# Expert places of 64 and 32 rows taken in two chunks of 1792 columns, and the places paired in another order

## The reference

```python
logits = xt @ w_router + b_router
top_v, top_i = lax.top_k(logits, 2)
gates = softmax(top_v)
combine = einsum('tk,tke->te', gates, one_hot(top_i, 8))
for e in range(8):
    out = out + combine[:, e:e+1] * ((silu(xt @ w_gate[e]) * (xt @ w_up[e])) @ w_down[e])
```

## Time and profile before

| | us |
|---|---|
| median of 3 runs (1421.67 to 1425.79) | 1423.94 |
| the profiled execution's own time | 1424.28 |
| its span | 1422.3 |
| TensorE busy | 1331.0 (94%) |
| VectorE busy | 466.4 (33%) |
| ScalarE busy | 279.3 (20%) |
| moved by DMA | 423.50 MB, mean 298 GB/s |

### The profile page before, as it was taken

The page is one execution under the profiler, slowest core; times in us unless marked ns, Lnnn a source line. Parts: engine busy times, 40 slices in busy tenths (PEclk is TensorE's granted clock), DMA queues, the critical chain, the costliest instruction groups (busy, mean ns, idle before and its releaser), DMA issues.

```text
span 1422.3 us, 18648 instructions
## 1 busy us (share of the span) xinstructions
PE 1331.0 (94%) x7762; PEld 753.4 (53%) x7762; DVE 466.4 (33%) x1035; ACT 279.3 (20%) x519; POOL 98.4 (7%) x115
## 2 busy tenths in 40 slices
PE   6989999999899979999999999999999999987775
PEld 5846599999684655454554444453433344332322
DVE  7998865554678541130101010110110100100002
ACT  3542444342263100000011010110110101000001
POOL 4530000000451000000000000000000000000000
PEclk9999999999899989999999999999999999999999
DMA  9433344438032288899999868989999999999994
GB/s 308 141 119 118 119 178 178 178 128 315 2 98 79 78 327 309 321 414 411 412 414 410 358 261 360 391 339 411 410 415 411 410 416 411 411 415 412 411 415 197
DMA packets 126734, 423.50 MB, mean 298 GB/s; under 512 B 21632, under 2 KB 23864, under 8 KB 118456
## 3 DMA queue, kind: packets, MB, share of 16 engines
q1 hardware_dynamic: 121464, 421.75, 75.7%
q10 hardware_dynamic: 5184, 0.52, 0.4%
HBM read 421.20 MB, written 1.05 MB: 297 GB/s over the span
## 4 chain that ended last, share of the span: by engine, by line
PE 74%; DMA 14%; DVE 8%; issue 1%; SPq 1%; ACT 1%; POOL 0%; DVEq 0%; ACTq 0%
PE psall L2349 14%; DMA m_ring<-in_moe_w_down_dram 12%; PE psall L2443 11%; PE psall L2364 8%; PE psall L2381 6%; PE psall L2054 4%; PE psall L2454 3%; PE psall L2269 3%; PE psall L2152 3%; PE psall L2271 3%; PE psall L2270 3%; PE psall L2218 2%; PE psall L2320 2%; PE psall L2481 2%; PE psall L2416 2%; PE psall L2251 1%
## 5 line engine op out<-in xcount | busy, mean ns | idle before, releaser
L2364 PE MATMUL psall<-m_ring,xeT 128*64 128x448 f32 x1024 | 202.5, 543 | 22.7 <-DMA m_ring<-in_moe_w_up_dram 21.6
L2443 PE MATMUL psall<-m_ring,hidT 128*64 128x512 f32 (+1 forms) x672 | 201.0, 597 | 17.1 <-DMA m_ring<-in_moe_w_down_dram 16.2
L2349 PE MATMUL psall<-m_ring,xeT 128*128 128x448 f32 x512 | 194.4, 540 | 0.0
L2364 PEld LDWEIGHTS psall<-m_ring,xeT 128*64 128x64 f32 x1024 | 73.5, 137 | 140.0 <-issue 139.0
L2349 PEld LDWEIGHTS psall<-m_ring,xeT 128*128 128x128 f32 x512 | 96.6, 190 | 92.4 <-issue 92.2
L2443 PEld LDWEIGHTS psall<-m_ring,hidT 128*64 128x64 f32 (+1 forms) x672 | 72.6, 154 | 136.2 <-issue 120.1
L1938 DVE TENSOR_TENSOR hid<-e_silu,psall 64x448 f32<-64x448 f32 x32 | 19.9, 623 | 354.6 <-ACT e_silu L1271 352.5
L1619 DVE TENSOR_TENSOR w_lo<-ring,w_hi 128x1024 fp32r<-128x1024 f32 x66 | 80.4, 1224 | 67.8 <-ACT w_hi L1215 67.8
L2381 PE MATMUL psall<-m_ring,xeT 128*32 128x448 f32 x1024 | 102.0, 542 | 0.0
L2269 PE MATMUL psall<-hnT_hi,w_hi 128*128 128x256 f32 x352 | 99.7, 283 | 0.7 <-DVE hnT_lo L1757 0.7
L2271 PE MATMUL psall<-hnT_hi,w_lo 128*128 128x256 f32 x352 | 99.5, 283 | 0.0
(11 more groups left out here) (327 smaller groups left out, 1454.7 us busy)
## 6 DMA issues: line engine op xcount, KB each, us to landing
m_ring<-in_moe_w_gate_dram SPq DMA_DIRECT2D x128, 896.0 KB, 20.1
m_ring<-in_moe_w_up_dram SPq DMA_DIRECT2D x128, 896.0 KB, 17.1
m_ring<-in_moe_w_down_dram SPq DMA_DIRECT2D x64, 1792.0 KB, 19.2
ring<-in_w_in_dram SPq DMA_DIRECT2D x10, 2048.0 KB, 12.8
ring<-in_ffn_w_gate_dram SPq DMA_DIRECT2D x5, 2048.0 KB, 10.4
ring<-in_ffn_w_up_dram SPq DMA_DIRECT2D x5, 2048.0 KB, 7.6
ring<-in_ffn_w_down_dram SPq DMA_DIRECT2D x5, 2048.0 KB, 7.8
ring<-in_w_out_dram SPq DMA_DIRECT2D x4, 2048.0 KB, 8.0
```

Of the source, the lines that this page charges most:

```text
L2349: ins = M(m_bank(key)[:, 0:MH], x[:, i, 0:P], weights(kind, i, s), start=(i == 0), stop=(i == KT - 1))
L2364: ins = M(m_bank(key)[64 * n:64 * n + 64, 0:MH], x[:, i, 0:64], weights(kind, i, s), start=(i == 0), stop=(i == KT - 1))
L2443: ins = M(y, hidT[:, r, 0:shape[0]], rows(r, 512 * n, 512), **ends)
```

## The change

Places of 64 and 32 rows (D and E) are now **narrow**: they have 2 chunks of 1792 columns instead of 4 of 896. A gate or up load of theirs is one row tile of 128 rows by 1792 columns, still one slot, so its rows are 7 KB instead of 3.5 KB; a turn of theirs has 16 slots of gate and up and 8 of down. The down loads keep their 14 KB rows, and A, B and C keep theirs of all kinds. The products are the same in number and size, but the side-by-side halves are now the two 896-column halves m of the chunk, and gate and up lie in banks of their own (`halves`, `halves_down`). So the hidden values of a D turn are 128 rows, of an E turn 64, and one set of 7 transposes serves a chunk of double width. The pairs are now (A,E), (D,D), (B,E), (C,D): "AEDDBECD". Turns: a pair whose first place is wide (A, B or C) goes 0,0,1,0,0,1, the pair (D,D) goes 0,1,0,1, 22 turns in all. The release of narrow units is one row tile of gate and up at a time. The path for further rows of an overfull expert (`NI`, not taken with this input) follows suit and is left out below.

```diff
-ITEMS = "AEBECDDD"
+ITEMS = "AEDDBECD"
...
+NARROW = 2
+MN = NARROW * MW
+TURNS = [(0, 1) * NARROW if CAPS[i] <= 64 else (0, 0, 1) * NARROW for i in range(0, NI, 2)]
+PICKS_AT = [1 if len(a) == 2 * NARROW else 2 for a in TURNS]
...
-        if pos == 2:
-            then = [("pt", p)]
-        if pos == 6 and 2 * p + 2 < NI:
-            first, then = [("xg", 2 * p + 2, 0)], [("xg", 2 * p + 2, 1)]
+        if pos == PICKS_AT[p]:
+            then = then + [("pt", p)]
+        if pos == FIRST_DONE[p] - 1 and 2 * p + 2 < NI:
+            first, then = first + [("xg", 2 * p + 2, 0)], then + [("xg", 2 * p + 2, 1)]
...
+    def narrow(self, it):
+        return self.shape(it) in ((64,), (32,))
+
+    def chunks(self, it):
+        return MC // NARROW if self.narrow(it) else MC
...
-        for base, rows in self.row_tiles(it):
+        for base, rows in [(0, NARROW * self.tokens(it))] if self.narrow(it) else self.row_tiles(it):
...
+        if self.narrow(it):
+            for i in range(KT - 1):
+                self.event(("kh", it, c, i))
+            if shape[0] == 64:
+                for kind, s, who, bank in (("g", 0, "A", 0), ("g", 1, "A", 1), ("u", 0, "V", 2),
+                                           ("u", 1, "V", self.misc())):
+                    self.add((kind, it, c, s), who, bank)
+            else:
+                for kind, who in (("g", "A"), ("u", "V")):
+                    self.add((kind, it, c, 0), who, self.rolling())
+            last = ("u", it, c, 1 if shape[0] == 64 else 0)
+            for i in range(KT):
+                for kind in "gu":
+                    self.load(it, c, kind, i, last if i == KT - 1 else ("kh", it, c, i))
+            return
...
+        if self.narrow(it):
+            for m in range(NARROW):
+                ends = keys and m == NARROW - 1
+                self.load(it, c, "d", 2 * m, ("dh", it, c, m))
+                self.load(it, c, "d", 2 * m + 1, keys[0] if ends else ("dn", it, c, m))
+                self.event(("dh", it, c, m))
+                if ends:
+                    self.add(keys[0], "A", keys[0][2])
+                else:
+                    self.event(("dn", it, c, m))
+            return
...
-                a = c * MW
+                narrow = experts.narrow(it)
+                a = c * (MN if narrow else MW)
                 if kind == "d":
+                    a, half = a + h // 2 * MW, h % 2
                     src = moe_w_down[0, e, a:a + MW, :].rearrange("e (p r) n -> p (e r n)", r=MB)
-                    sp.dma_start(unit(it, c, kind, h), src[:, h * DOWN * UNIT:(h + 1) * DOWN * UNIT]).then_inc(full, 16)
+                    sp.dma_start(unit(it, c, kind, h),
+                                 src[:, half * DOWN * UNIT:(half + 1) * DOWN * UNIT]).then_inc(full, 16)
+                elif narrow:
+                    src = (moe_w_gate if kind == "g" else moe_w_up)[0, e, h * P:(h + 1) * P, a:a + MN]
+                    sp.dma_start(unit(it, c, kind, h), src.rearrange("e p n -> p (e n)")).then_inc(full, 16)
...
+                if shape == (32,):
+                    m_arrived(act, ("g", it, c, 0), k)
+                    nc.scalar.activation(e_silu[:, 2, :], m_bank(("g", it, c, 0))[:, 0:MH],
+                                         ACT.Silu).then_inc(m_drained["A"], 1)
+                    return
...
+                    b = m_bank(("u", it, c, 0))
+                    for m in range(NARROW):
+                        for s in range(2):
+                            q = slice(64 * m + 32 * s, 64 * m + 32 * s + 32)
+                            ins = V.tensor_tensor(hid[32 * m:32 * m + 32, s * MH:(s + 1) * MH], e_silu[q, 2, :],
+                                                  b[q, 0:MH], ALU.mult)
+                    ins.then_inc(m_drained["V"], 1)
+                    return
...
+                def halves():
+                    one = 1 if shape[0] == 64 else 0
+                    for i in range(KT):
+                        tokens_in(i)
+                        for kind in "gu":
+                            unit_wait(pe, it, c, kind, i, k)
+                            w = unit(it, c, kind, i)
+                            for s in range(2):
+                                key = (kind, it, c, s * one)
+                                if i == 0 and (one or not s):
+                                    m_open(pe, key, k)
+                                for m in range(NARROW):
+                                    q = 64 * m if one else 64 * m + 32 * s
+                                    ins = M(m_bank(key)[q:q + shape[0], 0:MH], x[:, i, 0:shape[0]],
+                                            w[:, m * MW + s * MH:m * MW + (s + 1) * MH], start=(i == 0),
+                                            stop=(i == KT - 1))
+                                if i == KT - 1 and (one or s):
+                                    event(ins)
+                        if i < KT - 1:
+                            event(ins)
...
+                        if i < KT - 1:
+                            event(ins)
...
+            def halves_down(it, c, k):
+
+                n = experts.tokens(it)
+                lane = experts.lane(it)
+                last = c == experts.chunks(it) - 1
+                opens = c == 0 and not (n == 32 and lane and experts.shares(it))
+                wide = 512 if n == 64 else 256
+                for m in range(NARROW):
+                    for r in range(MB):
+                        if r in (0, 3):
+                            unit_wait(pe, it, c, "d", 2 * m + r // 3, k)
+                        ends = dict(start=(opens and m == 0 and r == 0), stop=(last and m == NARROW - 1 and r == MB - 1))
+                        for q in range(DM // wide):
+                            a = r * DM + q * wide
+                            big = DOWN * UNIT
+                            w = unit(it, c, "d", 2 * m + a // big)[:, a % big:a % big + wide]
+                            y = ps[5 + lane][64 * q:64 * q + 64, :] if n == 64 else \
+                                ps[7][32 * q:32 * q + 32, 256 * lane:256 * lane + 256]
+                            ins = M(y, hidT[:, r, n * m:n * m + n], w, **ends)
+                        if r in (3, MB - 1):
+                            event(ins)
```

More of the change, by code:

```diff
@@ L117, in __init__ @@
         self.add(("pt", NI // 2), "A", self.misc())
-        for c in range(MC):
+        for c in range(self.chunks(NI)):
             self.gate_up(NI, c)
@@ L122, in __init__ @@
             self.turned(NI, c)
-        self.down(NI, MC - 1)
+        self.down(NI, self.chunks(NI) - 1)
         self.scatter(NI // 2, range(4))
@@ L1262, in silus @@
                 shape = experts.shape(it)
+                if shape == (32,):
[3 more added lines that the diff above has]
+                    return
                 if shape[0] > 32:
                     for s in range(2):
-                        if shape[0] == P:
+                        if shape[0] == P or experts.narrow(it):
                             m_arrived(act, ("g", it, c, s), k)
@@ L1331, in _ @@
                     picks_out(NI // 2, k)
-                    for c in range(MC):
+                    for c in range(experts.chunks(NI)):
                         silus(NI, c, k)
@@ L1928, in hidden @@
                 shape = experts.shape(it)
+                if shape == (32,):
+                    m_wait_drained(dve, ("g", it, c, 0), k)
+                    m_arrived(dve, ("u", it, c, 0), k)
+                    b = m_bank(("u", it, c, 0))
[6 more added lines that the diff above has]
+                    return
                 for s in range(2):
                     cols = slice(s * MH, (s + 1) * MH)
-                    if shape[0] == P:
+                    if shape[0] == P or experts.narrow(it):
                         m_wait_drained(dve, ("g", it, c, s), k)
@@ L1972, in _ @@
                         choose(nxt, slice(nxt, nxt + 1))
[L1973 removed]
+                if pos == FIRST_DONE[p] - 1 and p + 1 < NI // 2:
                     take_tokens(2 * p + 2)
@@ L2385, in quad @@
                     return ins
-                if shape[0] == P:
+                if experts.narrow(it):
+                    halves()
+                elif shape[0] == P:
                     for kind in "gu":
@@ L2406, in hidden @@
                 shape = experts.shape(it)
-                last = ("w", it, c) if 32 in shape else ("u" if shape[0] == P else "gu", it, c, 1)
+                last = ("u", it, c, 0 if shape == (32,) else 1) if shape[0] == P or experts.narrow(it) else ("w", it, c)
+                if len(shape) > 1:
+                    last = ("w", it, c)
                 m_wait_drained(pe, last, k)
@@ L2424, in down @@
                 m_wait_drained(pe, ("tr", it, c, len(experts.r_pieces(it)) - 1), k)
-                last = c == MC - 1
+                last = c == experts.chunks(it) - 1
                 wide = shape[0] == P
+                if experts.narrow(it):
```

(4 more changed lines are left out.)

7 lines of the change are left out of this document (3 added, 4 removed).

## The result

The changed kernel takes **1416.58 us** (median of 4 runs, 1415.18 to 1418.49) beside 1424.49 for the kernel before in the same rounds (4 runs, 1421.67 to 1425.79): ratio **0.9942 [0.9927, 0.9957]**, 7.9 us or 0.6% faster. Forecast were 1416.8 us and a gain of 7.5. Three more measurements of the same loads and the same order, further down, give 0.9943, 0.9949 and 0.9933. The profiled execution is the longest of its four: its own time 1418.49 us, its span 1416.6.

A forecast was written before the change was run, and what follows sets the result against it. The kernel was taken as bound by a stream of loads with holes. Slots and holes gave -12.0 us, the tail +4.5, together -7.5 on the profiled 1424.28: 1416.8 us, range 1409 to 1429, chance 0.55.

The forecast's parts named there:

- 7 KB rows: Narrow gate and up loads: 418 GB/s, 2.194 us a slot against 2.265 in 3.5 KB rows; 8.8 us over 124 slots.
- the forecast's line: Load cost fitted from row lengths in the trace: 8.9 ns a packet plus 0.03703 ns a byte.
- 14 KB point: Input to the fit, from a stretch of mostly 14 KB rows: 425 GB/s, 539.7 ns per packet and engine.
- B's pair by TensorE: In (B,E) TensorE sets the pace: 203.6 us up to slot 83, holes 29.9 us against 31.2 before.
- Rival C: In B's pair TensorE finds loads missing and its chain grows: 1441 us at worst, halfway 1429; chance 0.12.
- The tail: Adding back the last pair, now (C,D) with two row tiles, takes 8.4 us instead of 3.91: +4.5 us.
- the ledger: Count of slots and holes from slot 35 to the stream's end: 811.3 us before, 799.3 after, difference -12.0.
- step b: From the end of the first D place's last down load to B's first product: 2.8 + 3.7 + 1.2 = 7.7 us.
- A load is still what comes last: In the last turn the final load, not TensorE, sets the end; margin 1 to 3 us, bounds 0 to +2.
- a sign against itself: At the kernel's end: the forecast would be wrong if the last load is not what `halves_down` waits for.
- Rival E, the clock at no cost: Granted clock is 1.00 in all windows but one (0.99), after starved stretches too: no cost; no chance given.
- time is slots, holes and tail; TensorE's idle time is no cost: Whole expert stage: time is slots times us per slot, plus holes, plus the tail behind the last load.

The follow-up runs named there:

- experiment 5: Changed kernel with each narrow chunk's 896-column halves taken far apart in memory, so gate and up loads have 3.5 KB rows: 1427.44 us, 1.0014 of the kernel before.
- experiment 7: The changed kernel measured again with nothing altered: 1417.88 us, 0.9949 of the kernel before.
- experiment 6: Changed kernel without the last pair's four products of row tile 1, leaving C's 32 extra rows out of the output: 1411.57 us, 0.9908 of the kernel before.
- experiment 4: Changed kernel with B's quad products moved in behind each up unit, so B's units come free pair by pair: 1421.51 us, 0.9968 of the kernel before.
- experiment 9: Changed kernel with the places in the order AECDBEDD, (C,D) second and (D,D) last: 1420.65 us, 0.997 of the kernel before.

## Why the prediction was right, and where it was not

- **7 KB rows: right, a size off.** Forecast 418 GB/s, measured 423 (a tenth and a fifth of it from 14 KB rows, which by the forecast's line adds 0.7 and 1.3). Most of the miss is in the forecast's 14 KB point: by the packets of that window 18% of its bytes are 3.5 KB rows. Taken out, 14 KB rows are at 430 GB/s and the line gives 421 for 7 KB, an estimate from the earlier trace rows, against some 422 for the measured windows treated alike (its 2 KB point is then 383 where the row says 386). The 3.5 KB rows gave 407.5, not 405. The effect, 0.083 us a slot where 0.071 was said, is shown by the same kernel with rows of both lengths, 9.6 us. By the rule of the Trainium skill (DMA: Bandwidth & Descriptors, Specifications) that 512 bytes suffice for line rate, experiment 5 would have changed nothing. The trace disagrees, 407 against 423 GB/s. By its fixed 3 cycles or so a packet (Why small descriptors are slow) the step would be 1.3%, an estimate; the runs show 3.8%.
- **B's pair by TensorE: right.** 81.2, 162.9, 201.8 us against 80.45, 162.5, 201.6; the holes 29.3 against 29.9. That the three times agree within 0.8 us is partly luck: 1.6 us of each is B1 at a low clock, and in experiment 7 they are 79.6, 161.3 and 200.1. Rival C, waits for loads in that pair, did not come: there is none.
- **The tail: right.** +4.6 us on the line, and experiment 6 shows it in the time.
- **The stream's end: about right.** The last bytes come 11.2 us earlier (1392.1 against 1403.3); the ledger said 12.0. With the tail's 4.6 and the 0.9 below, -11.2 + 4.6 + 0.9 = -5.7, which is what the profiled spans show (1416.6 - 1422.3). The forecast's 2.8 us from the end of the flow to the product that waited for it are 1.0 by the finer view (last bytes at 1403.3), so its step b was 1.8 too long.
- **The total: right, and in part luck.** 1416.8 was said of the profiled execution, which took 1418.49; what it meets within 0.2 us is the median of the four. The profiled one has two times of low clock that cost 3.2 us and are in no term. By the measure of experiment 7 the change is 867.1 - 879.9 = -12.8 us, with the tail -8.2, where -7.5 was said.
- **"A load is still what comes last": wrong**, by 0.9 us within the bounds of 0 to +2 that stood beside it. It is what the forecast named as a sign against itself. The step took 1 to 3 us of margin; C's `down` came with waits of 3.2 us, and from there TensorE had 22 us to go, with one wait of 1.60 for ScalarE's copy (1375.66 to 1397.67), more than the 16.4 us that the stream still needed.
- **Rival E, the clock at no cost: wrong, by 3.2 us in this execution.** A's second chunk takes 25.77 us instead of 24.22, B1's wide products 25.96 instead of 24.32. The granted clock is 0.50 (1.2 instead of 2.4 GHz) in each microsecond from 976 to 979 and full from 980; the first window below holds the end of that:

```profile
978.00:982.00 4.00, 4.00 (x10) 1.96 (x9) 0.00 (x0) 0.00 (x0) 0.00 (x0) 0.85 0.99 419
982.00:986.00 4.00, 4.00 (x12) 2.02 (x11) 0.00 (x0) 0.00 (x0) 0.00 (x0) 1.00 1.01 421
```

  Before, TensorE idled 38 us of the last 205 and could make such a loss good. Now the part behind 926 has next to no slack. The loss is not in three other executions (469.3, 469.4, 469.4 us against 470.9), but B1 has it in the traces of experiments 4 and 9.
- **The reading "time is slots, holes and tail; TensorE's idle time is no cost": half right.** As bookkeeping it held, for both kernels. As a cause it did not: the holes in B's pair are there because TensorE needs that long for the pair, and experiment 4, which let the units go earlier, changed where they lie and not how much the stream moved. In the new order the time is a sum of another kind: the stream up to B's first product (184 slots), then 469.4 us in which TensorE is busy 463, then the tail. Both sums come to the same end here because the stream and TensorE finish within 1 us of each other.
- **What the order is worth was never asked alone.** The forecast gave all gain to slots and holes in one ledger. Taken apart (changes of the ratio, across chips where they are not from one): the order alone +0.56%; the double chunks with it -0.42%; the 7 KB rows with them -0.65%. With narrow chunks the order makes no difference that the runs can tell (0.9954 and 0.9943; the profiled executions favour the new one by 2.3 us). So in the new order **the rows bring as much as the whole change and somewhat more**, and the double chunk about pays for the order. What rows and double chunks bring each in the old order was not run. That the double chunk removes just four slots of waiting ahead of B is read from two start times, 940.52 and 931.70; no run changed that number alone.

## What to carry to other kernels

Where a stream of loads bounds a kernel, fit ns per packet and per byte from the row lengths that the trace already has; the line foretold an unseen length within 1.2%. Count the row lengths in each window first, as a mixed window bends the line. Before spending an edit on holes, sum the compute engine's waits for loads behind them (here 3.2 us against 29 us of holes), for that is the most there is to win. And ask who makes the holes: where the compute engine is busy without a break and the ring is full, letting slots go earlier moves the holes about and brings no flow. When two bounds finish within a microsecond of each other, each further gain on one side must be asked of the other.

## What the runs showed of the hardware that was not expected

- Two adjacent pieces of 3.5 KB in one load's access pattern go out as one packet of 7 KB (106253 packets either way), and two pieces that lie apart as two (126733).
- Windows of mostly 7 KB rows move 423 GB/s, almost what one window of mostly 14 KB rows showed (425), and 3.8% more than 3.5 KB rows in the same places (407.5).
- The granted clock fell to 0.50 for 3.4 us at a time, amid work of TensorE. In the changed kernel's B1 it fell as B1's products began, behind an idle time of 0.85 us and 7 transposes; the same idle time is there in the three repeats, without the fall. In experiment 4 it also fell at 958, where TensorE had been busy without a pause since 918. Each time costs 1.6 to 1.7 us where TensorE has no slack.
- Executions of one kernel differ by up to 5 us in when the experts' first product starts (525.21 to 530.12), and by 0.2 us in what follows up to the last `down`, the low clock aside.
